# One decoder layer on one core: the fourth input sum moved ahead of the first column pair, and one small store moved from GpSimd's queue to SyncE's

## The reference, cut to what matters

```python
for l in range(DEPTH):                       # DEPTH = 1, SEQ = 1024, D_MODEL = 1024, D_FF = 2816
    x = x + 0.5 * swiglu(rmsnorm(x, ffn1_norm[l]), ffn1_w_gate[l], ffn1_w_up[l], ffn1_w_down[l])
    h = rmsnorm(x, mix_norm[l])
    sq, sk, sv, gq, gk, gv, gg, glr, mq = jnp.split(h @ w_in[l], splits, axis=-1)
    y_swa, y_gla, y_mem = ...                # windowed attention, gated linear attention, memory attention
    x = x + jnp.concatenate([y_swa, y_gla, y_mem], axis=-1) @ w_out[l]
    x = x + 0.5 * swiglu(rmsnorm(x, ffn2_norm[l]), ffn2_w_gate[l], ffn2_w_up[l], ffn2_w_down[l])

def swiglu(x, w_gate, w_up, w_down):
    return (jax.nn.silu(x @ w_gate) * (x @ w_up)) @ w_down
```

## Time and profile before

| what | value |
|---|---|
| median of three runs | 1784.29 us (1780.27 to 1785.05) |
| the profiled execution's own time | 1785.05 us |
| its span, first to last instruction | 1783.3 us |
| PE busy | 1712.8 us (96%) |
| DVE busy | 1134.3 us (64%) |
| ACT busy | 720.8 us (40%) |
| POOL busy | 536.1 us (30%) |
| mean granted clock of PE | 0.984 of full |

### The profile page before, as it was taken

How to read it: one execution, slowest core, us unless ns; L and a number is a source line. 1 busy time by engine, 2 the same in 40 slices (tenths; PEclk the granted TensorE clock), 3 DMA queues, 4 the chain that set the end, 5 groups by cost and what they waited for, 6 DMA issues and landing times. The chain is left out here.

```text
span 1783.3 us, 24793 instructions
## 1 busy us (share of the span) xinstructions
PE 1712.8 (96%) x8285; PEld 1389.3 (78%) x8285; DVE 1134.3 (64%) x1585; ACT 720.8 (40%) x1344; POOL 536.1 (30%) x437
## 2 busy tenths in 40 slices
PE   6999999999999999999999799799999999999999
PEld 4888888888778789877666578588888888877877
DVE  8975565555497684357778651896556545549654
ACT  5533333334244552142277721353333333334442
POOL 1454554343130231000056412044455434310000
PEclk9999999999999999999999889899999999999999
DMA  7142223324943340220100132104222332493334
GB/s 203 57 154 89 100 92 113 124 101 148 362 139 119 106 130 2 71 71 13 36 2 2 36 95 94 59 37 148 98 91 100 119 115 95 157 359 115 95 94 160
DMA packets 101693, 191.69 MB, mean 107 GB/s; under 512 B 11491, under 2 KB 13972, under 8 KB 101612
## 3 DMA queue, kind: packets, MB, share of 16 engines
q1 hardware_dynamic: 100528, 188.48, 31.4%
q0 software_dynamic: 848, 2.10, 0.8%
q10 hardware_dynamic: 236, 0.06, 0.0%
HBM read 139.74 MB, written 50.86 MB: 107 GB/s over the span
## 5 line engine op out<-in xcount | busy, mean ns | idle before, releaser
L474 DVE TENSOR_TENSOR ring<-w_raw,ring 128x512 fp32r<-128x512 f32 x240 | 238.1, 1007 | 219.6 <-ACT ring L469 219.5
L56 PE MATMUL ps<-hiT,ring 128*128 128x512 f32 x672 | 261.6, 389 | 0.5 <-ACT G L591 0.5
L58 PE MATMUL ps<-hiT,ring 128*128 128x512 f32 x672 | 261.4, 389 | 0.0
L56 PE MATMUL ps<-down_ring 128*128 128x512 f32 x616 | 241.6, 392 | 10.7 <-DVE down_ring L847 6.4
L57 PE MATMUL ps<-loT,ring 128*128 128x512 f32 x640 | 249.0, 389 | 0.0
L57 PE MATMUL ps<-down_ring 128*128 128x512 f32 x616 | 239.9, 389 | 0.0
L58 PE MATMUL ps<-down_ring 128*128 128x512 f32 x616 | 239.7, 389 | 0.0
L56 PE MATMUL ps<-hiB,ring 128*128 128x512 f32 x576 | 226.2, 393 | 9.5 <-DVE loB L360 9.5
L58 PE MATMUL ps<-hiB,ring 128*128 128x512 f32 x576 | 225.1, 391 | 0.0
L469 ACT ACTIVATE ring<-w_raw 128x512 fp32r<-128x512 f32 x240 | 150.3, 628 | 173.8 <-PE ps L58 160.5
L847 DVE TENSOR_TENSOR down_ring<-down_raw,down_ring 128x512 fp32r<-128x512 f32 x176 | 126.8, 731 | 123.5 <-ACT down_ring L843 123.3
(11 more groups left out here) (241 smaller groups left out, 3028.6 us busy)
## 6 DMA issues: line engine op xcount, KB each, us to landing
down_raw<-act_dram SPq DMA_DIRECT2D x154, 256.0 KB, 2.6
w_raw<-in_w_gate SPq DMA_DIRECT2D x88, 256.0 KB, 3.1
w_raw<-in_w_up SPq DMA_DIRECT2D x88, 256.0 KB, 3.2
act_dram<-actT SPq DMA_DIRECT2D x88, 256.0 KB, 2.0
wd<-in_w_down SPq DMA_DIRECT2D x88, 256.0 KB, 5.3
act_dram<-act SPq DMA_DIRECT2D x66, 256.0 KB, 2.0
p_raw<-in_w_proj SPq DMA_DIRECT2D x15, 512.0 KB, 3.5
xT<-in_x SPq DMA_DIRECT2D x8, 512.0 KB, 7.2
```

Source lines behind the costliest of these rows:

```text
L56: nc.tensor.matmul(out, w_hi, x_hi, start=first, stop=False, skip_group_check=resumed)
L58: return nc.tensor.matmul(out, w_lo, x_hi, start=False, stop=last, skip_group_check=resumed)
L474: nc.vector.tensor_tensor(ring[:, e % RING, 1, :], op_source(e), ring[:, e % RING, 0, :].bitcast(F32), ALU.subtract).then_inc(op_ready, 1)
```

## The change

It has three parts. First, T4's sum, its split and the second half's silus and products move from step 5 (and 6) of pair 1 into the head, ahead of the low split of operand 4 or 5. Second, in pair 1 all of ACT's `copy_x` of both banks wait until `acted` is 4, where before only the one into G22 did. Third, the store of `spans_raw` goes from POOL's queue to SP's, right behind the load of `masks_f`, with its wait for all 21 operations.

```diff
@@ head_scalar (ACT)
             hi("T1")
             ops(0, 1)
             hi("T2")
-            ops(2, 3, 4)
+            ops(2, 3)
             hi("T3")
+            ops(4)
+            hi("T4")
+            head_silu(act, f, 1, 0, G12)
+            head_silu(act, f, 1, 1, G22)
@@ ffn_scalar (ACT)
             def copy_x(i, x, done, dst, free):
                 n = b.pair + i
-                if dst is G22 and isinstance(i, int) and i == 1:
+                if isinstance(i, int) and i == 1:
                     free = 4
...
-                    if first and s == 5:
-                        head_silu(act, f, 1, 0, G12)
-                        head_silu(act, f, 1, 1, G22)
-                        for j in range(KK):
-                            split_hi(act, f, "T4", j)
@@ head_vector (DVE)
             sums(sum_t2)
             ops(2, 3)
             lo("T2")
+            sums(sum_t4)
+            lo("T3")
             ops(4)
-            lo("T3")
+            lo("T4")
+            head_gated(dve, f, 1, 0, G12, act12)
+            head_gated(dve, f, 1, 1, G22, act22)
@@ ffn_vector (DVE)
                     evict(i, s)
-                    if first and s == 5:
-                        for j in range(KK):
-                            sum_t4(dve, f, j)
-                        head_gated(dve, f, 1, 0, G12, act12)
-                        head_gated(dve, f, 1, 1, G22, act22)
                     op(i, s, last)
-                    if first and s == 6:
-                        for j in range(KK):
-                            split_lo(dve, f, "T4", j)
@@ down_sync (SP)
                 sp.dma_start(masks_f[:], masks_in).then_inc(masks_landed, 16)
+                sp.wait_ge(span_built, 3 * SPLITS)
+                sp.dma_start(spans_dram, spans_raw[:]).then_inc(spans_stored, 16)
@@ spans_pool (POOL)
-            pool.wait_ge(span_built, 3 * SPLITS)
-            pool.dma_start(spans_dram, spans_raw[:]).then_inc(spans_stored, 16)
```

## The result

The changed kernel takes 1815.55 us as the median of four runs (1814.97 to 1815.79), against 1783.49 for the kernel before in four runs. The ratio is 1.0174, with a 95% interval of 1.0155 to 1.0193: 32 us slower. The forecast was 1818, from 1805 to 1829. The profiled execution took 1817.94 us with a span of 1816.1, where before it was 1785.05 and 1783.3: the two traces are 32.8 us apart. Seven further executions of the changed kernel are on record, from 1808.76 to 1817.31 us; the lowest is still 24 us above the kernel before.

The account below looks back on a forecast made before the run. PE, busy 96% of the span, was taken as the bound, so new waits reaching it cost time. Stalls 8.8 + 8.6 + 10.2 plus 6.0 clock restart made 33.6 us on 1784.29: 1818 us, range 1805 to 1829.

Parts of the forecast that it names:

- stall before e = 4, f = 0: First SwiGLU layer's head: PE waits for DVE's late add_y, 8.8 us idle, bounds 6.0 to 9.5.
- stall before e = 4, f = 1: Second layer's head: the same wait for add_y, 8.8 - 0.2 = 8.6 us.
- stall before step 16: First down pass: load_b(33) queued behind SP's wait for POOL's table, 10.2 us, bounds 8.4 to 17.3.
- half clock behind the three: After each stall PE restarts at half clock, 1.4 to 2.6 us each; 6.0 us in all, between 4.2 and 7.8.
- the replay of DVE: Head, from 69.04 us: four sums slowed by POOL, products end at 82.5, add_y at 88.9 after operands 5 to 8.
- the case the prediction priced at 7.7: Head, behind the products: DVE keeps ahead of POOL, operands 5 and 6 pass undisturbed, stall 7.7 us instead of 8.8.
- the sign: Expected in the trace: PE idle once before e = 4 in each SwiGLU layer, 8 to 9 us, released by add_y.
- Part 2 "costs nothing of its own": Pair 1: ACT's copies wait for all four products until 82.5, adding no cost while DVE is the later one.
- Part 3: Before step 16: SP free at 504.3, load_b(33) issued at 504.8 and landed at 508.4; step 16 10.2 us later.
- The rival that POOL keeps its pace: Spans table: POOL's small operations stay at 0.74 us, so the store's move costs 17.3 us; 1825 us, chance 0.08.
- No rival: Rivals: only SP's wait counts, 0.07; only the head counts, 0.04; POOL keeps its pace, 0.08; not slower, 0.05.
- the rival "not slower": Stretch 466.37 to 499.63: store leaves GpSimd's queue, reloads stay hidden, at most 3.9 us gained; 1780 to 1784, chance 0.05.

Follow-up runs that it names:

- adds_first: head_copies_early with both add_y of pair 1 (and operand 5's low split) done among the moved work: 1787.25 us, ratio 1.0009 to the kernel before.
- sp_store_alone: The kernel before with only the spans store moved to SP's queue, directly behind the load of masks_f: 1796.88 us, ratio 1.0078.
- sp_store_later: The kernel before with the spans store on SP's queue behind load_b(61) instead of the load of masks_f: 1785.39 us, ratio 1.0000.
- head_copies_early: The changed kernel with the spans store back on POOL's queue and ACT's pair 1 copies waiting as in the kernel before: 1800.2 us, ratio 1.0086.

## Why the prediction was right, and where it was not

| term | predicted | measured in the trace |
|---|---|---|
| stall before e = 4, f = 0 | 8.8 | 7.1 |
| stall before e = 4, f = 1 | 8.6 | 7.45 |
| stall before step 16 | 10.2 | 10.4 |
| half clock behind the three | 6.0 | 2.45 + 2.2 + 1.6 = 6.25 |
| sum | 33.6 | 31.2 |

**Part 1, the replay of DVE, held, with some luck in the first layer.** The products were put at 82.5 and ended at 82.46 (81.19 + 1.27); POOL began its sums at 82.55. That this agrees to 0.04 us is luck. The replay starts the four sums at 69.04, "up to which nothing changes", and gives them four slow places. In the trace they start at 67.88, 1.16 us earlier, and T3's first split is slow too, 1.1 us more; the two cancel. PE and POOL were 0.5 us later in this run's head, so the slow place fell on T3's splits and not on T2's. In the second layer the steps are the replayed ones, 13.5 us from the first sum to the end of the products:

```profile
1202.75 6.88 DVE L337 TENSOR_TENSOR rawT<-rawT,rawB 128x512 f32<-128x512 f32 x4
1209.55 2.49 DVE L360 TENSOR_TENSOR loT<-rawT,hiT 128x512 fp32r<-128x512 f32 x4
...
1214.97 1.28 DVE L424 TENSOR_TENSOR act<-ps,G 128x512 f32<-128x512 f32 x2
```

adds_first shows that the cause is the order, as the prediction said. What was mis-sized is the last stretch, three splits at 1.70 behind a first one that is free. Operand 6's split passed at 0.6 as well, which is the case the prediction priced at 7.7 from the 4.03 us row and did not take; and in the first layer PE itself stood 0.5 us later (e = 0 at 69.75 instead of 69.25), which took that much off the stall. So PE idled about 7 us and not the 8 to 9 given as the sign.

**Part 2 "costs nothing of its own" was the step that failed.** The prediction looked only at whether ACT would be the last before `add_y`. It is not; but its late high part of operand 7 ends at 83.68 (83.06 + 0.62), when DVE has just finished operand 6's low split at 83.67. The three splits of 4.02 us, in two views:

```profile
82.99 0.68 DVE L474 TENSOR_TENSOR ring<-w_raw,ring 128x512 fp32r<-128x512 f32 x1
83.71 3.30 DVE L474 TENSOR_TENSOR ring<-w_raw,ring 128x512 fp32r<-128x512 f32 x2
```

DVE pauses, POOL takes the port, and the next two splits stand behind it. Undoing that one condition took 2.1 and 2.9 us off the idle times (behind the products it is 2.1 us in each layer) and brought POOL's first sum from 2.25 to 3.46 us. So 4 to 5 us of what the prediction booked under part 1 hang on part 2.

**Part 3 held in each step.** POOL alone was estimated at 0.31 for 64 columns and 0.45 for 128 from the fit through the earlier trace rows; 64 columns took 0.29. SP was free 8.70 us behind POOL's start (513.71 - 505.01), where 9.0 was worked out; the reload needed 3.8 from issue to ACT (518.24 - 514.46), where 3.6 was. The rival that POOL keeps its pace falls. sp_store_alone confirms the size and sp_store_later the cause.

**The clock.** 1.4 to 2.6 us a stall from the earlier trace rows holds all three. No run took the clock's part away while leaving the stalls; it is read from the lengths of the groups behind them.

**No rival happened.** Both stalls and all three waits were there, and nothing later gave back.

## What to carry to other kernels

When work is moved ahead on an in-order engine, list what the other engines wait for behind it and find the smallest margin; here `add_y` had 0.6 us and ten instructions went before it. A wait on a DMA queue for another engine's result belongs where that result has long been there: the same store cost 12 us in one place and nothing that can be measured 15 reloads later. And when a queue is full, order its transfers by when they are needed, which was worth 0.4% here (about 7.5 us), more than the 3.9 us that the rival "not slower" allowed the change at most.

## What the runs showed of the hardware that was not expected

DVE and POOL do not simply take turns at the port. POOL's first sum, 1.29 us alone, took 2.25 when DVE paused after two splits, 3.46 when DVE ran four without a pause (head_copies_early), and 4.08 when it ran five (adds_first). In each of them it ended 1.13 to 1.16 us behind the end of the last split that had held it off: 84.80 behind 83.67, 86.18 behind 85.04, 88.55 behind 87.39. So DVE kept the port for as long as its splits followed one another without a gap, and a split that started 0.12 us late (83.71 instead of 83.59) was enough to lose it. `add_y`, which reads PSUM, did not keep it: in head_copies_early POOL's sum ran beside it. Once POOL had the port, its back-to-back sums and DVE's splits alternated at about 1.7 us. The Trainium skill (SBUF - State Buffer, section "Who interferes with whom") has the exclusive lock, and the trace agrees; that a run of DVE instructions holds off a waiting POOL instruction is what these runs add.
